# Expert weights laid out and moved in one 8192 B piece per partition

## What is computed

```python
# 32 experts; each token goes to 2 of them; blocks of 128 rows per expert
xb = xt[row_tok].reshape(n_blocks, MOE_BLOCK, D)          # D = 1024
def expert_block(args):
    xblk, eid = args
    hid = jax.nn.silu(xblk @ w1[eid]) * (xblk @ w3[eid])  # w1, w3: 1024 x 512
    return hid @ w2[eid]                                  # w2: 512 x 1024
yb = lax.map(expert_block, (xb, blk_expert)).reshape(R, D)
y = jnp.zeros((N, D)).at[row_tok].add(yb * row_gate[:, None])
```

## Time and profile before

| | |
|---|---|
| median of the runs | 2226.5 us |
| the profiled execution's own time | 2225.1 us |
| its span | 2223.4 us |
| TensorE matmul busy | 2070.6 us (93%) |
| VectorE, ScalarE busy | 1185.8 us (53%), 937.2 us (42%) |
| loads of expert weights | 192, 1 MiB each |
| DMA traffic | 397.09 MB, 125145 packets |

### The profile page before, as it was taken

How to read it: one execution, slowest core, us unless ns; L and a number is a source line. 1 busy time by engine, 2 the same in 40 slices (tenths; PEclk the granted TensorE clock), 3 DMA queues, 4 the chain that set the end, 5 groups by cost and what they waited for, 6 DMA issues and landing times.

```text
span 2223.4 us, 27808 instructions
## 1 busy us (share of the span) xinstructions
PE 2070.6 (93%) x10578; PEld 1746.1 (79%) x10578; DVE 1185.8 (53%) x1409; ACT 937.2 (42%) x1189; POOL 218.7 (10%) x278
## 2 busy tenths in 40 slices
PE   6999999999999999999599999998799999999980
PEld 6988888887888888888489877787688888888860
DVE  4105333111343334341366767634888888888856
ACT  5223122221233333232234534412477777777752
POOL 0000000001111020200000000000122222222210
PEclk9999799999999999999699999998799999999995
DMA  4111113223223142320522356414699999999945
GB/s 164 47 51 57 51 64 141 96 106 142 90 98 123 73 148 76 140 93 39 189 78 75 135 176 230 148 78 175 237 361 373 381 390 386 383 384 377 376 177 236
DMA packets 125145, 397.09 MB, mean 179 GB/s; under 512 B 15025, under 2 KB 36033, under 8 KB 119122
## 3 DMA queue, kind: packets, MB, share of 16 engines
q1 hardware_dynamic: 107038, 351.81, 42.2%
q0 software_dynamic: 18016, 44.00, 5.6%
HBM read 343.13 MB, written 69.40 MB: 186 GB/s over the span
## 4 chain that ended last, share of the span: by engine, by line
PE 78%; issue 7%; DVE 7%; DMA 5%; ACT 2%; POOLq 1%; SPq 0%; POOL 0%; DVEq 0%; ACTq 0%
PE psum L606 21%; PE psum L607 20%; PE psum L608 20%; PE psum L2071 3%; DMA e_raw<-in_w_e 2%; PE psum L2201 2%; PE psum L2186 2%; PE psum L2096 1%; DMA rows<-rows_scratch 1%; PE psum L2419 1%; PE psum L2038 1%; DVE e_l L1876 1%; DMA expert_rows<-yb,aidx 1%; PE psum L2345 1%; PE psum L2032 1%
## 5 line engine op out<-in xcount | busy, mean ns | idle before, releaser
L1876 DVE TENSOR_TENSOR e_l<-e_raw,e_h 128x2048 fp32r<-128x2048 f32 x190 | 424.9, 2285 | 37.9 <-ACT e_h L1219 37.4
L606 PE MATMUL psum<-hT_h,w_l 128*128 128x512 f32 x1088 | 440.0, 404 | 0.0
L608 PE MATMUL psum<-hT_h,w_h 128*128 128x512 f32 x1088 | 429.8, 395 | 0.0
L607 PE MATMUL psum<-hT_l,w_h 128*128 128x512 f32 x1088 | 429.7, 395 | 0.0
L1219 ACT CAST e_h<-e_raw 128x2048 fp32r<-128x2048 f32 x190 | 354.6, 1929 | 32.2 <-DMA e_raw<-in_w_e 20.6
L1327 DVE TENSOR_TENSOR w_l<-wraw,w_h 128x2048 fp32r<-128x2048 f32 (+1 forms) x38 | 87.0, 2289 | 300.5 <-ACT w_h L924 300.5
L608 PEld LDWEIGHTS psum<-hT_h,w_h 128*128 128x128 f32 x1088 | 207.8, 191 | 45.4
L606 PEld LDWEIGHTS psum<-hT_h,w_l 128*128 128x128 f32 x1088 | 208.4, 192 | 41.6
L607 PEld LDWEIGHTS psum<-hT_l,w_h 128*128 128x128 f32 x1088 | 208.5, 192 | 40.7
L606 PE MATMUL psum<-e_h,xT_l 128*128 128x512 f32 x512 | 203.8, 398 | 5.0 <-DVE xT_l L1882 4.8
L965 ACT COPY stage<-psum 128x512 f32<-128x512 f32 x96 | 56.4, 588 | 342.9 <-PE psum L608 342.9
(11 more groups left out here) (362 smaller groups left out, 3381.6 us busy)
## 6 DMA issues: line engine op xcount, KB each, us to landing
e_raw<-in_w_e SPq DMA_DIRECT2D x192, 1024.0 KB, 9.4
wraw<-in_w_in_t SPq DMA_DIRECT2D x37, 1024.0 KB, 4.8
pt_scratch<-stage SPq DMA_DIRECT2D x52, 512.0 KB, 2.6
gate<-pt_scratch SPq DMA_DIRECT2D x24, 512.0 KB, 3.8
rows<-rows_scratch SPq DMA_DIRECT2D x8, 1280.0 KB, 8.3
h_scratch<-xn SPq DMA_DIRECT2D x16, 512.0 KB, 3.6
yg<-expert_rows SPq DMA_DIRECT2D x8, 1024.0 KB, 13.1
conv_scratch<-co POOLq DMA_DIRECT2D x12, 512.0 KB, 2.9
```

The source lines that it names most:

```text
L606: nc.tensor.matmul(out_ap, ll, rh, start=first, stop=False)
L607: nc.tensor.matmul(out_ap, lh, rl, start=False, stop=False)
L608: return nc.tensor.matmul(out_ap, lh, rh, start=False, stop=last)
L1876: nv.tensor_tensor(e_l[:, c], e_raw[:, c], e_h[:, c].bitcast(F32), ALU.subtract).then_inc(s_el13 if c < 4 else s_el2, 1)
```

## The change

The host lays each chunk out with a partition's two halves side by side, and the load then takes 8192 B per partition in one piece in place of two pieces of 4096 B. What arrives in `e_raw` is the same.

```diff
             def load_chunk(b, e, c):
-                src = w_e[bass.ds(e, 1), c].rearrange("a s p f -> p (a s) f")
-                sp.dma_start(e_raw[:, c].rearrange("p (s f) -> p s f", s=2), src).then_inc(s_er[c], 16)
+                src = w_e[bass.ds(e, 1), c].rearrange("a p f -> p (a f)")
+                sp.dma_start(e_raw[:, c], src).then_inc(s_er[c], 16)
...
 def layout_experts(w1, w3, w2):
 
-    out = np.empty((w1.shape[0], 6, 2, P, D), np.float32)
+    out = np.empty((w1.shape[0], 6, P, 2, D), np.float32)
     for at, w in ((0, w1), (2, w3)):
-        out[:, at:at + 2] = w.reshape(-1, 2, 2, 2, P, NC).transpose(0, 1, 2, 4, 3, 5).reshape(-1, 2, 2, P, D)
-    out[:, 4:6] = w2.reshape(-1, 2, 2, P, D)
-    return out
+        out[:, at:at + 2] = w.reshape(-1, 2, 2, 2, P, NC).transpose(0, 1, 4, 2, 3, 5).reshape(-1, 2, P, 2, D)
+    out[:, 4:6] = w2.reshape(-1, 2, 2, P, D).transpose(0, 1, 3, 2, 4)
+    return out.reshape(-1, 6, P, 2 * D)
```

## The result

The changed kernel takes 2252.25 us (median of 4 runs, 2247.36 to 2254.29) against 2226.61 us beside it: a ratio of 1.0116, 95% interval 1.0098 to 1.0134. That is 25.6 us more; 16.7 were forecast. Its profiled execution has a span of 2251.0 us, 27.6 more than before.

What follows compares the result with a forecast made beforehand. TensorE bounds the expert phase, with GpSimd's serial loop almost as long. Lost blocks +17, tail +1, stalls removed -1.3 give +16.7 us: 2241.8, as median 2243 us; own range 2231 to 2252, 8-in-10 range 2219 to 2262.

Steps and rivals of the forecast that it cites:

- What bounds the kernel, and the lack of slack: Expert phase: TensorE bounds at 17.83 us per block; GpSimd's gather-scatter loop takes 17.80 us, 1.4 us to spare.
- The creep and TensorE's stalls go: Expert phase: weight landings stop creeping from 7.1 to 11.8 us, and TensorE's 1.3 us of stalls go.
- The load gets cheaper: Weight loads: 48 pieces of 0.310 us replace 96 of 0.161, 0.58 us less per block and DMA engine.
- The rows' traffic: Gather and scatter pieces each wait behind one longer weight piece: 1.34 us scatter, 0.67 gather, 2.0 us per block.
- The queue ahead: Weight pieces queued before a row DMA's first piece: taken as 0 added, upper end +1.8 us per DMA.
- rival C: Much slower: 12 pieces stay ahead, now of 8192 B; block about 19.7 us, 2273 us; with all above 2252, chance 0.15.
- The relief: Expert phase: as blocks lengthen and DMA share falls to 0.93, the two landings sum to 14.9 us, not 16.0.
- The sum: Block about 18.6 us; 21 of 28 gathers cost 0.8 us each, +17; tail +1, stalls -1.3: +16.7 us.
- The signs: Expert-phase trace: TensorE waits for rows each block from about the eighth, transposes 18.3 to 19 us apart, scatter 9 to 10.
- B: Rival, no change: GpSimd's loop lengthens by less than its slack, 2222 to 2231 us; chance 0.24.
- A: Rival, faster: no turns by the piece, only relief of the DMA backlog, about 2221 or 2219 us; chance 0.25.

Runs made afterwards that it cites:

- e5: Changed kernel (8192 B pieces) with GpSimd's drain between row-index copy and indirect DMA replaced by a semaphore: 2220.11 us, ratio 0.9976.
- e6: Kernel before (4096 B pieces) with GpSimd's drain between row-index copy and indirect DMA replaced by a semaphore: 2224.02 us, ratio 0.9995.
- e9: Changed kernel with ScalarE's copies of the result rows moved behind the hidden high part and first down chunk: 2254.95 us, ratio 1.0132.
- e2: Weight loads in four pieces of 2048 B per partition, against the kernel before with 4096 B: 2236.17 us, ratio 1.0049.

## Why the prediction was right, point by point

**What bounds the kernel, and the lack of slack.** Right. The block of TensorE is the bound before; with GpSimd's loop longer than it, the block is 1.4 us longer. One reading was off: that the loop "depends on nothing else". The waits before, 1650 to 2100 us, also have

```profile
POOL bidx L865 <- PE psum L2419: 9.3, 9, 3.6
```

GpSimd waited for TensorE's transposes in every block up to 1770 us, less each time, and in the last three for under 1 us. Up to 1770 us the loop was the shorter one and tied to the block; only from then on did the two run side by side.

**The creep and TensorE's stalls go.** Right: loads land in 7.9 us at the end, and ScalarE's waits for them are gone.

**The load gets cheaper, 0.58 us per block.** Not seen in the engines' busy time. Per load it is, from 1650 to 2100 us, 0.860 x 450 / (147.15 / 1.049) = 2.76 us after (147.15 MB at 86.0%), and 0.918 x 450 / (157.75 / 1.049) = 2.75 us before: nothing. Where TensorE keeps its pace, e5 against e6, it is 2.69 against 2.73 (158.74 MB at 90.4% and 158.96 MB at 92.1%), 0.3 us per block; without scatters 2.72 against 2.82, the full 0.6. Yet the two prices hold: the median piece in this stretch takes 0.309 us (8192 B) and 0.159 us (4096 B), beside other traffic as alone. What they leave out are the first pieces of a load that finds its queue empty, which the packet records show at up to about 1 us each. The earlier trace rows lie in the middle of a load and miss them. Whole loads with almost nothing beside them in the kernel before, 8192 B (57.5 to 60.9 us) and 4096 B (1564.4 to 1568.2 us):

```profile
q1 hardware_dynamic: 132, 1.05, 87.1%
...
q1 hardware_dynamic: 272, 1.05, 86.4%
```

That is 3.4 x 0.871 = 2.96 and 3.8 x 0.864 = 3.28 us of each engine, against 8 x 0.310 = 2.48 and 16 x 0.161 = 2.58. The long pieces add 0.28 us to a load in the changed kernel and 0.19 in the kernel before (mean piece against median piece).

**The rows' traffic, 1.34 us for the scatter and 0.67 for the gather.** Right in sum. From first row piece to last, the scatter takes 1.4 us longer and the gather 0.5: 1.9 against 2.0. But the turn that it was worked out from, one weight piece for one row piece, is not what the runs show: the earlier trace rows has 1.7 weight packets to a row piece, the changed kernel 1.5. (1.61 MB / 8192 B x 0.310 - 0.94 MB / 4096 B x 0.161) / 16 = 1.5 us is the same work read from the rows. That 9 x 0.149 comes so near is in part luck.

**The queue ahead, taken as 0.** Held, and rival C with it: the scatter is not at 12 us. The records speak against a fixed number of pieces held ahead: the gather's first piece comes 4.2 us after its issue both in e6 (4096 B) and in e5 (8192 B), with the engines as full, where 12 pieces would have made it 1.8 us later.

**The relief.** This is the term that failed in size. I let the two landings give back 1.1 us as the DMA share fell to 0.93, by the stretch at the earlier trace rows. The share is 0.94, and what comes earlier is the first row piece, by 0.3 us for the scatter (5.4 to 5.2) and 0.5 for the gather (4.2 to 3.6): some 0.8. In the stretch of 1900 to 1960 us the net is 9.8 + 7.8 - 16.0 = 1.6 us where 0.9 was forecast, over 1650 to 2100 us it is 17.5 - 16.4 = 1.1; the block, 19.2 us and not 18.6, lies between the two. What made the early landings of the earlier trace rows, at the share of the earlier trace rows, so short is not settled: GpSimd still waited for TensorE there and its DMAs were not back to back, but in the same blocks of the changed kernel, at a share of 0.95, they are 9.1 and 9.3 us.

**The sum.** The slack was used up as said, only sooner: the pace changes after the fourth block of the windows above, not after seven. The sum let the first gathers land in 8.2 us, and they took 9.1. 25 blocks x 1.37 = 34 us in place of 21 x 0.8 = 17. The tail came out 1.6 us shorter, not 1 longer. So the loop's own loss, 32.8 us with the stalls taken off, is twice the 15.7 of the sum; that the total is nearer (27.6 us in the profiled execution, 25.6 by the medians, against 16.7) is owed to 5.2 us of early start and shorter tail that nobody forecast, and is luck. The median of 2252.25 us lies a quarter of a us above the upper edge of the forecast's own range (2231 to 2252) and inside the whole one.

**The signs.** Scatter at 9 to 10 us, loads at 7 to 8 us without a creep, DMA share 0.92 to 0.95, half the packets: all came. The transposes are 19.2 us apart, above the 18.3 to 19 given. And TensorE does wait for the gathered rows, but in 12 blocks and for 5.9 us; its more frequent wait comes through the scatter, ScalarE's `yb` and VectorE, which the prediction did not name. e9 shows that this is secondary: with it gone the block is as long.

**The rivals.** B fell with the block at 19.2 us. A fell too. e5 comes out at 2220 us, in the 2219 to 2221 that A gave, but not by A's relief: without the drain TensorE keeps 17.82 us with 4096 B as well. The Trainium skill, in Perfetto Trace Analysis (DMA Optimizations), says that larger pieces can improve throughput dramatically, and names this for kernels bound by DMA. The engines' share agrees where both forms keep TensorE's pace (91.6 against 94.8% without scatters); the time of this kernel, bound by TensorE and then by GpSimd's loop, does not. The Trainium skill, in DMA: Bandwidth & Descriptors (Queues, rings and completion order), says that an engine drains a whole packet, some 9 to 17 descriptors, before it changes queues. By that a load's share would be one packet before and after and the scatter's service would have stayed at 3 us; it is 4.6 above, so this case speaks against it, though e2 shows that the turns are not by single piece either.

## What to carry to other kernels

Here the piece size of a full DMA queue also set how long another queue's pieces took to be served (3.0 to 4.4 us for a scatter). Before enlarging pieces, look for small transfers on the same engines whose landing somebody waits for. A loop on an engine off the critical path can be as long as the block; here, once it was, 1.3 us more of landings cost 1.4 us per block. Compare the periods of all loops with the bound's and not only their idle shares. Once the drain between index copy and indirect DMA was gone, the same change was harmless: 2220.11 us, faster than both kernels, while the form with 4096 B and no drain, 2224.02 us, can't be told from the kernel before, nor clearly from the 8192 B form.

## What the runs showed of the hardware

- A drain on GpSimd also waits for the indirect DMA that it issued before. With it each indirect DMA came after the landing of the last one, after an idle time of 7.2 to 7.5 us in the rows of the changed kernel; without it the scatter was issued 4.8 us after the gather, with 0.27 us idle.
- Piece size acts on the other queue, though not in proportion. The same 144 row pieces took 3.1 us of service beside pieces of 2048 B, 3 us beside 4096 B, 4.6 us beside 8192 B, whether 41 or 108 of them were real rows (kernel before). A view of the kernel before, a gather into empty engines (1575.3 to 1577.6 us), suggests that there is a floor, though no run tested it: alone they spread over some 2.3 us with the engines two fifths busy.

```profile
q0 software_dynamic: 144, 0.27, 39.9%
```

- A load that starts on an empty queue costs its engines more than its pieces in the middle tell: 2.96 us for 128 pieces of 8192 B, against 8 x 0.310 = 2.48 by the earlier trace rows. In the changed kernel, beside other traffic, it is 2.76 us.
- A gather of 128 rows landed 4.2 us after its issue in empty engines and 7.6 us after it beside the full loads' queue. By the packet records 1.7 and 4.2 us of that pass before the first row piece is served.
